# One all-engine barrier at the end of each phase, with GpSimd's semaphore clears after it: a two-layer hybrid decoder kernel

## The chip, the core and the metric

The kernel runs on one core of a Trainium2 chip. A core has five engines that run their own instruction streams and meet only at semaphores: TensorE (PE; its weight loads are listed as PEld), VectorE (DVE), ScalarE (ACT), GpSimd (POOL) and SyncE (SP), which here issues nearly all DMA transfers. The metric is the device time of one execution in microseconds (us), less is better. Durations of single instructions and waits come from one profiled execution of the kernel before.

## What is computed

Two causal decoder layers over a sequence of 1024 tokens, width 1024. Layer 0 mixes tokens with chunked gated linear attention (GLA), layer 1 with a dilated window attention in three head groups; beside each mixer runs a cross-attention into 256 memory tokens; each layer ends with a gated MLP. Cut to what matters:

```python
def reference(x, mem, ...):
    mem_n = rms_norm(mem, mem_norm)
    for i in range(DEPTH):                      # DEPTH = 2
        h = rms_norm(x, mix_norm[i])
        if i % 4 == 0:
            tok, xq = gla_mixer(h, a_w_in, a_w_gate2, a_b_gate, a_o_norm)
        else:
            tok, xq = dilated_mixer(h, b_w_in, b_q_norm, b_k_norm, positions)
        xa = memory_cross_attention(xq, mem_n, xa_w_kv[i], xa_q_norm[i], xa_k_norm[i])
        x = x + jnp.concatenate([tok, xa], axis=-1) @ w_out
        x = x + conv_ffn(rms_norm(x, ffn_norm[i]), ffn_w_up[i], ffn_conv_w[i], ffn_conv_b[i],
                         ffn_w_down[i])
    return x
```

All products are of float32 quality: a helper `split_matmul` (lines 50 to 52) makes each of three matmuls, high by high, high by low and low by high part.

## The kernel before

The program is a chain of twelve **phases**, each a Python function called from `build`, that follow each other in time: `project_phase` p0 (layer 0's input projection, with the memory's keys and values), `gla_phase`, `out_phase` o0 (output projection and norm), `ffn_phase` f0, then for layer 1 three pairs of `project_phase` p1_0, p1_1, p1_2 and `attention_phase` da0, da1, da2 (one pair per dilation), `out_phase` o1 and `ffn_phase` f1.

In each phase every engine has its own program, written inside one `nc.Block()`. Within a phase the engines are ordered by semaphores, one per kind of event (a tile loaded, split, turned, added). They only count up, and each phase counts from zero, so a phase's semaphores have to be back at zero before their numbers are handed out again. The allocator goes round the numbers, so that a number freed by one phase comes up again only after many others. Line 40 makes such a semaphore and leaves its clear as work for the end of the phase:

```python
def phase_semaphore(nc, ctx, name):
    s = ctx.enter_context(nc.semaphore(name))
    ctx.callback(nc.gpsimd.sem_clear, s)
    return s
```

What `ctx`, an `ExitStack`, does when the phase's `with` ends runs in the reverse of the order in which it was entered. So the end of a phase is: first the end of the `nc.Block()`, which is itself an all-engine barrier; then one clear on GpSimd for each semaphore of the phase; and last what was entered first, which before the change is `nc.all_engine_barrier`. A barrier has two halves: each engine drains and adds to a gather semaphore, GpSimd waits for the four others and then raises a release semaphore on which each of them waits (an EVENT_SEMAPHORE in the trace, whose start is the moment of the release). All of this has the line of the `with` that ends: L869 in a projection, L1396 in the GLA phase, L565 in an output phase, L82 in an MLP phase, L1141 in an attention phase. Two more `ExitStack`s have a barrier of their own: `c4` around p0 (L2405, 30 clears of the opening, the rope tables and the first parts), and `slots_ctx` around layer 1's weight slots (L2474, 6 clears, closed between p1_2 and da2).

What stands at a phase's start matters as well. In the GLA phase GpSimd first fills a mask `gla_keep` (L1563), which VectorE reads in a scan (L1705). At the end of da2 SyncE stores the last logarithms of the softmax sums, `group_lse<-stage_lse` (L2278), without waiting for them; o1 begins with SyncE waiting for that store and loading all three groups back, `o_logs<-group_lse` (L1944), with ScalarE issuing the load of the norm's gain, and with VectorE splitting two weight chunks (`o_w_lo`, L515), which wait for that gain, and then merging the groups (`o_top`, L1965, up to `XY`, L1988), for which TensorE waits.

Of the kernel before, what the change touches and what calls it, by code (L numbers as in the profile page):

```python
# [37 lines left out]


def phase_semaphore(nc, ctx, name):  # L40

    s = ctx.enter_context(nc.semaphore(name))
    ctx.callback(nc.gpsimd.sem_clear, s)
    return s
# [33 lines left out]
def ffn_phase(nc, ph, psum, ident, neg_half, X, hT_hi, hT_lo, w_up, conv_w, conv_b, w_down, x_out, raws, up, next_gain=None, next_w=None):  # L78
# [1 line left out]


    with ExitStack() as ctx:  # L82
        ctx.callback(nc.all_engine_barrier)
        def sb(name, shape, dt=F32):
            return ctx.enter_context(nc.sbuf_tensor(f"{ph}_{name}", shape, dt))

# [474 lines left out]
def out_phase(nc, ph, psum, ident, neg_half, XY, weights, x_dram, gain, out_hi, out_lo, w_up, up, raws, stage=None):  # L561
# [1 line left out]

    chunks, w_split = weights.chunks, weights.split
    with ExitStack() as ctx:  # L565
        ctx.callback(nc.all_engine_barrier)
        def sb(name, shape, dt=F32):
            return ctx.enter_context(nc.sbuf_tensor(f"{ph}_{name}", shape, dt))

# [263 lines left out]
def project_phase(nc, ph, psum, ident, neg_half, blocks, slots, extra_loads=(), guest=None, saves=None,  # L833
# [33 lines left out]
            n_heads += blk["kind"] == "heads"  # L867

    with ExitStack() as ctx:  # L869
        ctx.callback(nc.all_engine_barrier)  # L870
        def sb(name, shape, dt=F32):
            return ctx.enter_context(nc.sbuf_tensor(f"{ph}_{name}", shape, dt))

# [257 lines left out]
def attention_phase(nc, ph, psum, ident, units, stage=None, loads=(), load_unit=0, ahead=None, room=()):  # L1131
# [7 lines left out]
    U = len(units)  # L1139
    staged = TT * DIL_HEADS if stage is not None else 0  # L1140
    with ExitStack() as ctx:  # L1141
        ctx.callback(nc.all_engine_barrier)
        def sb(name, shape, dt=F32):
            return ctx.enter_context(nc.sbuf_tensor(f"{ph}_{name}", shape, dt))

# [239 lines left out]
def gla_phase(nc, ph, psum, ident, neg_half, hT_hi, hT_lo, w_in, w_gate2, b_gate, rank_rows, V, Y, room, first_parts, last_rows, cross_room, pieces,  # L1385
# [8 lines left out]
    DK, DV, PAIRS, CH = GLA_DK, GLA_DV, SEQ // P, SEQ // CHUNK  # L1394
    LAST = GLA_HEADS - 1
    with ExitStack() as ctx:  # L1396
        ctx.callback(nc.all_engine_barrier)
        def sb(name, shape, dt=F32):
            return ctx.enter_context(nc.sbuf_tensor(f"{ph}_{name}", shape, dt))

# [889 lines left out]
def build(nc, a, out):  # L2290

    with ExitStack() as ctx:
# [67 lines left out]
        with ExitStack() as c:  # L2360
# [11 lines left out]
            with ExitStack() as c2:  # L2372
# [12 lines left out]
                with ExitStack() as c3:  # L2385
                    slots = WeightSlots(nc, c3, "w0", B)

                    keys = [raws.tiles[1][:, :].rearrange("p (h n) -> p h n", h=XA_HEADS), sb("keys1", [P, XA_HEADS, N_MEM], F32, c3)]
                    vals = [raws.tiles[0][:, i * D // 2:(i + 1) * D // 2].rearrange("p (c n) -> p c n", c=2) for i in range(2)]
                    mem_parts = mem_hi, mem_lo  # L2390
                    def key_dest(i):
                        def dest(t, src):
                            s = src.rearrange("p (a n) -> p a n", n=P)
                            tok = slice(t * P, (t + 1) * P)
                            return [(keys[i][0:64, 0:XA_HEADS:2, tok], s[0:64, :, :]), (keys[i][64:P, 1:XA_HEADS:2, tok], s[64:P, :, :])]
                        return dest

                    kv_blocks = []
                    for i in range(2):
                        wkv = a["xa_w_kv"][i, :, :]  # L2400
                        kv = dict(tiles=N_MEM // P, stat=mem_parts, pick=plain)
                        kv_blocks += [dict(kind="heads", dim=XA_DIM, gain=xa_gain[i][1][:, :], w=wkv[:, 0:D_XA], dest=key_dest(i), **kv),
                                      dict(kind="copy", w=wkv[:, D_XA:2 * D_XA], dest=lambda t, i=i: vals[i][:, t, :], **kv)]
                    blocks[2:2] = kv_blocks
                    with ExitStack() as c4:  # L2405
                        c4.callback(nc.all_engine_barrier)
                        saves = [(keys_d[i], keys[i][:, :, :].rearrange("p h n -> p (h n)")) for i in range(2)]
                        saves += [(vals_d[i], vals[i][:, :, :].rearrange("p h n -> p (h n)")) for i in range(2)]

                        first = FirstParts(nc, c4, w, [XY[:, :, D_MIX + i * P:D_MIX + (i + 1) * P] for i in range(2)], qk_hi, qk_lo)  # L2410
                        rope = Rope(nc, c4, a["positions"], a["inv_freq"], XY[:, :, D_MIX:], *rope_d, first)
                        opening = Opening(
                            nc, c4, psum, ident, neg_half, band, split, zeros, [k[:, :, :] for k in keys],
                            [(xa_gain[i][j][:, :], a[f"xa_{n}_norm"][i, :]) for i in range(2) for j, n in enumerate("qk")]
                            + [(o_gain[:, :], a["a_o_norm"]), (dil_gain[0][:, :], a["b_q_norm"]), (dil_gain[1][:, :], a["b_k_norm"])],
                            a["mem"][0, :, :], a["x"][0, :, :], XY, [V[:, :, B + i * P:B + (i + 1) * P] for i in range(2)],
                            [xqT[:, i, :].rearrange("p (d n) -> p d n", d=DC) for i in range(2)], a["mem_norm"], a["mix_norm"][0, :],
                            *mem_parts, h0_hi, h0_lo)
                        project_phase(nc, "p0", psum, ident, neg_half, blocks, slots, guest=rope, saves=(5, saves), opening=opening)
# [22 lines left out]
        with ExitStack() as c:  # L2442
            cos, sin = sb("cos", [P, TT, DIL_DIM // 2], F32, c), sb("sin", [P, TT, DIL_DIM // 2], F32, c)
            rope_loads = [(x[:, :, :].rearrange("p t k -> p (t k)"), d) for x, d in zip((cos, sin), rope_d)]
            qT, kT = (sb(f"dil_{n}T", [P, DIL_HEADS, SEQ], F32, c) for n in "qk")
            V = XY[:, :, 0:D_DIL]
            XQ = XY[:, :, D_DIL + D_XA:]
            slots_ctx = c.enter_context(ExitStack())
            slots_ctx.callback(nc.all_engine_barrier)
            slots = WeightSlots(nc, slots_ctx, "w", HALF, raws)  # L2450

            def head_dest(x):
                return lambda t, src: [(x[:, :, t * P:(t + 1) * P], src.rearrange("p (h n) -> p h n", n=P))]

            def group_blocks(g):

                off, r = g * D_DIL, DILATIONS[g]
                blocks = [dict(whole, kind="heads", dim=DIL_DIM, gain=dil_gain[i][:, :], rope=(cos, sin), w=w[:, i * cols + off:i * cols + off + D_DIL],
                               pick=plain, dest=head_dest(x)) for i, x in enumerate((qT, kT))]
                return blocks + [dict(whole, kind="copy", w=w[:, 2 * cols + off:2 * cols + off + D_DIL],  # L2460
                                      pick=lambda x, d, t: tokens(x[:, d, :], t, r), dest=lambda t: V[:, t, :])]

            for g, r in enumerate(DILATIONS):
                blocks = group_blocks(g)
                if g == 0:
                    blocks.insert(0, dict(whole, kind="heads", dim=XA_DIM, gain=xa_gain[1][0][:, :], w=xq_w,
                                          pick=plain, dest=lambda t, src: [(XQ[:, t, :], src)]))
                project_phase(nc, f"p1_{g}", psum, ident, neg_half, blocks, slots, rope_loads if g == 0 else (),
                              room=raws.tiles)
                with ExitStack() as c2:  # L2470
                    if g + 1 < len(DILATIONS):
                        ahead = SlotsAhead(slots, group_blocks(g + 1)[0]["w"])
                    else:
                        slots_ctx.close()  # L2474
                        ahead = weights = OutWeights(nc, c1, "o1", (D_DIL + D_XA) // P, a["b_w_out"], raws, 3)
                    units = []
                    for t in range(TT):
                        for h in range(DIL_HEADS):
                            k, n, first = keys_of(kT[:, h, :], t, r)
                            mask = split[:, :] if r == 16 else band[:, 2 * P - n:2 * P]  # L2480
                            units.append((tokens(qT[:, h, :], t, r), k, n, mask,
                                          [V[:, first + i, h * P:(h + 1) * P] for i in range(n // P)],
                                          stage.tile[t % 2][:, h * P:(h + 1) * P], float(DIL_DIM) ** -0.5))
                    loads = ()
                    if g == 0:
                        keys, vals = xa_keys(1, c2)
                        loads = xa_loads(1, keys, vals)
                        units += xa_units(lambda h, t: XQ[:, t, h // 2 * P:(h // 2 + 1) * P], keys, vals, D_DIL)
                    attention_phase(nc, f"da{g}", psum, ident, units, stage, loads, TT * DIL_HEADS,
                                    ahead=ahead, room=raws.tiles if g + 1 < len(DILATIONS) else ())  # L2490
# [33 lines left out]
```

## Time and profile before

| what | us |
|---|---|
| median of 3 runs | 2705.37 (2704.56 to 2706.03) |
| the profiled execution's own time | 2706.76 |
| its span, first to last instruction | 2704.9 |
| TensorE (PE) busy | 2596.7 (96%) |
| VectorE, ScalarE, GpSimd busy | 1317.2, 845.6, 185.9 |
| mean granted TensorE clock | 0.98 |

The span is read against the profiled execution's own time, which is 1.9 us longer, and that again lies 1.4 us above the median of the runs. Semaphore instructions, drains and clears don't count as busy, so a stretch in which every engine only waits at a barrier shows as a stretch without any busy time.

### The profile page before, as it was taken

What the parts mean: (1) busy time and instruction counts of PE and PEld (TensorE: products, weight loads), DVE (VectorE), ACT (ScalarE), POOL (GpSimd) and SP (SyncE); (2) the same over time, 40 slices, a digit from 0 to 9 for tenths busy, and PEclk for the clock granted to TensorE, in tenths of its full rate; (3) what the DMA queues carried; (4) which work ended last, traced back from release to release, by engine and by line L of the source; (5) the groups of instructions that cost most, each with busy time, mean ns of one, the idle gap of its engine ahead of it and who ended that gap; (6) DMA issues with size and microseconds to landing.
All of it is one profiled execution on the core that took longest, in us unless ns stands there. A gap on an engine that the chain in (4) does not pass through costs nothing. (4 is left out here: it accounts for less than half of the span.)

```text
span 2704.9 us, 33076 instructions
## 1 busy us (share of the span) xinstructions
PE 2596.7 (96%) x12444; PEld 2201.6 (81%) x12444; DVE 1317.2 (49%) x2306; ACT 845.6 (31%) x1782; POOL 185.9 (7%) x263
## 2 busy tenths in 40 slices
PE   7998888999999999998999999997999999999999
PEld 7997767888888888887888888796778888888887
DVE  4423463354445555545545553443645444544455
ACT  6434342332222222224326433324332222222221
POOL 1100120000000000002211111111000000000000
PEclk9999898999999999998999999998999999999999
DMA  4221301131111111102102001103421111111111
GB/s 145 89 71 26 99 6 50 36 96 47 47 47 51 50 47 47 47 32 101 58 6 75 32 32 55 55 16 103 140 65 55 60 49 47 49 52 47 47 39 63
DMA packets 165245, 153.88 MB, mean 57 GB/s; under 512 B 32856, under 2 KB 135496, under 8 KB 165128
## 3 DMA queue, kind: packets, MB, share of 16 engines
q1 hardware_dynamic: 160968, 152.31, 17.7%
q8 instruction: 72, 1.18, 0.2%
q10 hardware_dynamic: 4160, 0.02, 0.1%
q14 instruction: 45, 0.37, 0.1%
HBM read 134.69 MB, written 17.61 MB: 56 GB/s over the span
## 5 line engine op out<-in xcount | busy, mean ns | idle before, releaser
L356 PE MATMUL psum<-hT_hi,f_up_hi 128*128 128x512 f32 x1376 | 426.7, 389 | 4.6 <-PEq L565 3.9
L356 PE MATMUL psum<-hT_hi,f_up_lo 128*128 128x512 f32 x1376 | 426.3, 389 | 0.0
L356 PE MATMUL psum<-hT_lo,f_up_hi 128*128 128x512 f32 x1376 | 426.2, 389 | 0.0
L238 DVE TENSOR_TENSOR f_up_lo<-raw,f_up_hi 128x1024 fp32r<-128x1024 f32 x84 | 102.9, 1225 | 490.6 <-ACT f_up_hi L182 490.6
L356 PEld LDWEIGHTS psum<-hT_hi,f_up_hi 128*128 128x128 f32 x1376 | 258.1, 188 | 59.4 <-issue 5.9
L356 PEld LDWEIGHTS psum<-hT_hi,f_up_lo 128*128 128x128 f32 x1376 | 258.3, 188 | 53.8
L356 PEld LDWEIGHTS psum<-hT_lo,f_up_hi 128*128 128x128 f32 x1376 | 258.3, 188 | 53.6
L256 DVE TENSOR_TENSOR XY<-XY,psum 128x512 f32<-128x512 f32 x352 | 234.4, 684 | 113.9 <-PE psum L52 113.7
L182 ACT ACTIVATE f_up_hi<-raw 128x1024 fp32r<-128x1024 f32 x84 | 89.1, 1061 | 614.6 <-PE psum L356 589.0
L50 PE MATMUL psum<-w_hi,hT_hi 128*128 128x512 f32 (+1 forms) x640 | 250.0, 391 | 17.0 <-DVE w_lo L808 10.5
L50 PE MATMUL psum<-f_down_hi,f_act_hi 128*128 128x512 f32 x640 | 249.0, 389 | 0.0
L51 PE MATMUL psum<-f_down_lo,f_act_hi 128*128 128x512 f32 x640 | 249.0, 389 | 0.0
L52 PE MATMUL psum<-f_down_hi,f_act_lo 128*128 128x512 f32 x640 | 249.0, 389 | 0.0
L52 PE MATMUL psum<-w_hi,hT_lo 128*128 128x512 f32 (+1 forms) x640 | 246.1, 385 | 0.0
L51 PE MATMUL psum<-w_lo,hT_hi 128*128 128x512 f32 (+1 forms) x640 | 246.0, 384 | 0.0
L50 PEld LDWEIGHTS psum<-w_hi,hT_hi 128*128 128x128 f32 x640 | 138.8, 217 | 35.7 <-DVE w_lo L808 10.1
L52 PEld LDWEIGHTS psum<-w_hi,hT_lo 128*128 128x128 f32 x640 | 138.8, 217 | 18.1
L51 PEld LDWEIGHTS psum<-w_lo,hT_hi 128*128 128x128 f32 x640 | 139.1, 217 | 16.7
L52 PEld LDWEIGHTS psum<-f_down_hi,f_act_lo 128*128 128x128 f32 x640 | 120.1, 188 | 25.0
L51 PEld LDWEIGHTS psum<-f_down_lo,f_act_hi 128*128 128x128 f32 x640 | 120.1, 188 | 24.9
L50 PEld LDWEIGHTS psum<-f_down_hi,f_act_hi 128*128 128x128 f32 x640 | 120.1, 188 | 24.9
L50 PE MATMUL psum<-w_hi,h_hi 128*128 128x384 f32 (+1 forms) x320 | 106.1, 332 | 2.3 <-DVE h_lo L475 1.7
(296 smaller groups left out, 4019.5 us busy)
## 6 DMA issues: line engine op xcount, KB each, us to landing
raw<-in_ffn_w_up_dram SPq DMA_DIRECT2D x88, 512.0 KB, 3.7
f_down_raw<-in_ffn_w_down_dram SPq DMA_DIRECT2D x22, 1024.0 KB, 4.9
w_raw<-in_b_w_in_dram SPq DMA_DIRECT2D x18, 1024.0 KB, 5.0
w_raw<-in_a_w_in_dram SPq DMA_DIRECT2D x8, 768.0 KB, 5.8
group_out<-stage SPq DMA_DIRECT2D x24, 256.0 KB, 2.3
o_outs<-group_out SPq DMA_DIRECT2D x24, 256.0 KB, 3.5
XY<-in_x_dram SPq DMA_DIRECT2D x8, 512.0 KB, 10.2
w_raw<-in_xa_w_kv_dram SPq DMA_DIRECT2D x8, 512.0 KB, 3.6
```

The lines of the kernel that those rows point to most:

```text
L50: nc.tensor.matmul(out, lhs_hi, rhs_hi, start=start, stop=False)
L51: nc.tensor.matmul(out, lhs_hi, rhs_lo, start=False, stop=False)
L52: return nc.tensor.matmul(out, lhs_lo, rhs_hi, start=False, stop=stop)
L182: nc.scalar.activation(up_hi[n_slot][:, :, :], up_raw[n_slot], ACT.Copy).then_inc(up_high, 1)
L238: nc.vector.tensor_tensor(up_lo[n_slot][:, :, :], up_raw[n_slot], up_hi[n_slot][:, :, :].bitcast(F32), ALU.subtract).then_inc(up_split, 1)
L256: nc.vector.tensor_tensor(xs, xs, psum[:, 4 + i % 4, :], ALU.add).then_inc(x_added, 1)
L356: mm = nc.tensor.matmul(psum[:, 2 * j + half, :], w[j][:, d, :], h[:, d, half * HALF:(half + 1) * HALF], start=first, stop=final)
```

## The change

The seven lines that leave a barrier as the last thing of a scope go. Two of them are in scopes that `build` opens once, five in phase functions that are called twelve times in all, so that 14 barriers leave the program. The barrier that ends each `nc.Block()` stays, and so do all 265 clears, in the same order on GpSimd: 21 of them end the program, and 17 (of scopes that had no barrier of their own: 6 behind p0, 6 behind o0, 5 behind o1) stand behind the last barrier of their place in the program before, too.

```diff
@@ def ffn_phase, gla_phase, out_phase, project_phase, attention_phase
     with ExitStack() as ctx:
-        ctx.callback(nc.all_engine_barrier)
         def sb(name, shape, dt=F32):
...
@@ def build
                     with ExitStack() as c4:
-                        c4.callback(nc.all_engine_barrier)
                         saves = [(keys_d[i], keys[i][:, :, :].rearrange("p h n -> p (h n)")) for i in range(2)]
...
             slots_ctx = c.enter_context(ExitStack())
-            slots_ctx.callback(nc.all_engine_barrier)
             slots = WeightSlots(nc, slots_ctx, "w", HALF, raws)
```

No instruction that computes or moves data changes its place on any engine; what goes is seen where an instruction waits for the barrier's gather semaphore. On GpSimd, between its last work of p0 (the norm's `p_head_rstd`) and its first of the GLA phase, an ISA row being one or more clears, the program before reads:

```order
L1017 TENSOR_TENSOR p_head_rstd<-p_head_sums,neg_half 128x4 [waits p0_mean]
L869 UNCONDITIONAL_BRANCH
L869 ISA [waits barrier_Pool_Activation_PE_DVE_SP_gather]
L869 ISA x12
L2405 ISA [waits barrier_Pool_Activation_PE_DVE_SP_gather]
L2405 ISA x29
L2385 ISA [waits barrier_Pool_Activation_PE_DVE_SP_gather]
L2385 ISA x5
L1561 UNCONDITIONAL_BRANCH
L1563 MEMSET gla_keep 96x1024
```

and the changed program at the same place:

```order
L1016 TENSOR_TENSOR p_head_rstd<-p_head_sums,neg_half 128x4 [waits p0_mean]
L869 UNCONDITIONAL_BRANCH
L869 ISA [waits barrier_Pool_Activation_PE_DVE_SP_gather]
L869 ISA x12
L2402 ISA x30
L2382 ISA x6
L1558 UNCONDITIONAL_BRANCH
L1560 MEMSET gla_keep 96x1024
```

Three barriers became one, the first; the 49 clears stand behind it, and no other engine waits for them. Between da2 and o1 the program before has, again on GpSimd, 11 clears (L1141) between two barriers:

```order
L547 TENSOR_TENSOR o_w_lo<-raw,o_w_hi 128x1024 [waits gla_xa_turned]
L1141 UNCONDITIONAL_BRANCH
L1141 ISA [waits barrier_Pool_Activation_PE_DVE_SP_gather]
L1141 ISA x10
L654 UNCONDITIONAL_BRANCH [waits barrier_Pool_Activation_PE_DVE_SP_gather]
L431 TENSOR_SCALAR o_norm_sums<-o_norm_sums 128x1 [waits gla_k_parked]
```

and the changed one has the same without the second wait (semaphores stand under the first name that their number had):

```order
L548 TENSOR_TENSOR o_w_lo<-raw,o_w_hi 128x1024 [waits gla_xa_turned]
L1140 UNCONDITIONAL_BRANCH
L1140 ISA [waits barrier_Pool_Activation_PE_DVE_SP_gather]
L1140 ISA x10
L654 UNCONDITIONAL_BRANCH
```

## Rows read from the trace of the kernel before

**Rows 1.** The page: span, and its first section, busy time per engine.

```profile
span 2704.9 us, 33076 instructions
PE 2596.7 (96%) x12444; PEld 2201.6 (81%) x12444; DVE 1317.2 (49%) x2306; ACT 845.6 (31%) x1782; POOL 185.9 (7%) x263
```

**Rows 2.** Instructions of line L1396, end of GLA: count, ns, first and last start.

```profile
L1396 POOLq EVENT_SEMAPHORE_RANGE_CLEAR  x38: 44/44/44, 412.3 to 415.2; - x38
L1396 PEldq EVENT_SEMAPHORE  x2: 51/51/51, 412.3 to 415.5; - x2
```

**Rows 3.** Windows between first and last release: length, busy per engine, PEclk, DMA share, GB/s.

```profile
216.70:220.30 3.60, 0.00 (x0) 0.00 (x0) 0.00 (x0) 0.00 (x0) 0.00 (x0) 0.75 0.00 0
412.30:415.50 3.20, 0.00 (x0) 0.00 (x0) 0.00 (x0) 0.00 (x0) 0.00 (x0) 0.50 0.01 3
533.50:534.90 1.40, 0.00 (x0) 0.00 (x0) 0.00 (x0) 0.00 (x0) 0.00 (x0) 1.00 0.00 0
1259.10:1261.30 2.20, 0.00 (x0) 0.00 (x0) 0.00 (x0) 0.00 (x0) 0.00 (x0) 0.50 0.00 0
1433.20:1434.40 1.20, 0.00 (x0) 0.00 (x0) 0.00 (x0) 0.00 (x0) 0.00 (x0) 1.00 0.00 0
1509.00:1510.00 1.00, 0.00 (x0) 0.00 (x0) 0.00 (x0) 0.00 (x0) 0.00 (x0) 1.00 0.00 0
1651.60:1652.80 1.20, 0.00 (x0) 0.00 (x0) 0.00 (x0) 0.00 (x0) 0.00 (x0) 1.00 0.00 0
1698.90:1699.90 1.00, 0.00 (x0) 0.00 (x0) 0.00 (x0) 0.00 (x0) 0.00 (x0) 1.00 0.26 8
1844.60:1846.80 2.20, 0.00 (x0) 0.00 (x0) 0.00 (x0) 0.00 (x0) 0.00 (x0) 0.98 0.00 0
1881.00:1882.10 1.10, 0.00 (x0) 0.00 (x0) 0.00 (x0) 0.00 (x0) 0.00 (x0) 0.50 0.48 158
1989.30:1991.20 1.90, 0.00 (x0) 0.00 (x0) 0.00 (x0) 0.00 (x0) 0.00 (x0) 1.00 0.00 0
sum 20.00, PE 0.00 PEld 0.00 DVE 0.00 ACT 0.00 POOL 0.00; mean PE 0.00 PEld 0.00 DVE 0.00 ACT 0.00 POOL 0.00
```

**Rows 4.** Instructions of lines L82 and L2292, the program's end.

```profile
L82 PEldq EVENT_SEMAPHORE  x2: 51/51/51, 2703.2 to 2704.8; - x2
L82 POOLq EVENT_SEMAPHORE_RANGE_CLEAR  x19: 44/44/44, 2703.2 to 2704.5; - x19
...
L2292 POOLq EVENT_SEMAPHORE_RANGE_CLEAR  x2: 44/44/44, 2704.8 to 2704.9; - x2
```

**Rows 5.** Instructions that write or read the tile gla_keep.

```profile
L1705 DVE TENSOR_TENSOR_SCAN raw<-gla_keep,gla_soft x4: 2287/2287/2287, 238.8 to 348.9; 96x1024 f32<-96x1024 f32 x4
L1563 POOL MEMSET gla_keep<- x1: 947/947/947, 220.8 to 220.8; 96x1024 f32 x1
```

**Rows 6.** The start of o1: DMA issues by line, line L1944, and the timeline.

```profile
group_lse<-stage_lse SPq DMA_DIRECT2D x1, 16.0 KB, 1.9
...
L1944 SPq DMA_DIRECT2D o_logs<-group_lse x3: 372/576/770, 1882.2 to 1883.2; - x3
DMA to landing us min/median/max: 2.9/3.1/3.5
...
1885.59 2.36 DVE L515 TENSOR_TENSOR o_w_lo<-raw,o_w_hi 128x1024 fp32r<-128x1024 f32 x2 [5.74 <-DMA o_gain<-in_ffn_norm_dram]
1887.87 0.18 DVE L1965 TENSOR_TENSOR o_top<-o_logs 128x32 f32<-128x32 f32 x1
```

**Rows 7.** Windows at half TensorE clock behind five boundaries, and one at full clock.

```profile
220.30:225.40 5.10, 5.02 (x16) 3.77 (x17) 0.00 (x0) 1.06 (x2) 1.07 (x2) 0.50 0.54 108
1437.10:1440.50 3.40, 3.40 (x12) 2.83 (x13) 1.46 (x11) 1.72 (x6) 0.00 (x0) 0.50 1.02 378
...
sum 22.10, PE 21.70 PEld 18.13 DVE 6.75 ACT 9.53 POOL 5.09; mean PE 4.34 PEld 3.63 DVE 1.35 ACT 1.91 POOL 1.02
...
534.90:540.00 5.10, 4.95 (x22) 4.12 (x23) 0.00 (x0) 0.00 (x0) 0.00 (x0) 1.00 0.27 42
```

More of the change, by code:

```diff
@@ L565, in out_phase @@
     with ExitStack() as ctx:
-        ctx.callback(nc.all_engine_barrier)
         def sb(name, shape, dt=F32):
@@ L869, in project_phase @@
     with ExitStack() as ctx:
-        ctx.callback(nc.all_engine_barrier)
         def sb(name, shape, dt=F32):
@@ L1141, in attention_phase @@
     with ExitStack() as ctx:
-        ctx.callback(nc.all_engine_barrier)
         def sb(name, shape, dt=F32):
@@ L1396, in gla_phase @@
     with ExitStack() as ctx:
-        ctx.callback(nc.all_engine_barrier)
         def sb(name, shape, dt=F32):
```

## The prediction, made before the change was timed

> **What bounds the kernel now.** I read the page first. TensorE is busy 96% of a span of 2704.9 us, and GpSimd 7% [rows 1]. With one engine so full, what a barrier costs is not the work of the barrier but the time in which TensorE cannot be fed; so the question is how long the whole core stands still at each of the twelve phase ends, and how much of that is the second barrier.
>
> The next view was the list of instructions by line, for the lines of the `with` statements. It lists semaphore instructions as well, though they don't count as busy. At the end of the GLA phase TensorE's queue is released twice, at 412.3 and at 415.5, and between the two GpSimd runs 38 clears that start from 412.3 to 415.2 [rows 2]. So one clear takes 2.9 / 37 = 0.08 us of GpSimd's time, though its own record is 44 ns long, and the barrier behind them takes 415.5 - 415.2 = 0.3 us with the last clear. The same reading at each other boundary gives a first and a last release, and the third view, the busy time in windows, was asked for just those stretches: in all eleven no engine has any busy time at all [rows 3]. They sum to 20.0 us. The stretches are as long as their clears are many: 3.6 us at the end of p0 (13 + 30 clears, two barriers), 1.0 to 1.2 us at the ends of projections and attentions.
>
> The reader is to see that everything of the next phase stands behind the last release. A stretch in which nothing works and nothing is awaited but the release can go completely, and everything after it moves earlier by its length.
>
> **The change part by part.**
>
> *The eleven inner boundaries.* After the change engines go on at the first release. Taken off: 3.6 + 3.2 + 1.4 + 2.2 + 1.2 + 1.0 + 1.2 + 1.0 + 2.2 + 1.1 + 1.9 = 20.0 us [rows 3], if nothing else holds the next phase back.
>
> *What could be awaited instead: a transfer.* If a DMA is under way in the stretch and its data is needed first, its landing doesn't move. The DMA share is 0.00 or 0.01 in nine of the eleven stretches; it is 0.26 at the end of da1 and 0.48 at the end of da2 [rows 3]. The one at da1 is again a store of that group's logarithms, which is read back only in o1, so nothing there waits. At da2 it matters: the store `group_lse` lands 1.9 us after it is issued, and SyncE's first load of `o_logs` starts at 1882.2, right with the last release at 1882.1 [rows 3, 6]. SyncE was held by the store about as long as by the barrier, and it will still start these three loads near 1882.2 to 1883.2. The last of them lands 2.9 to 3.5 us after its issue, at 1886.1 to 1886.7. VectorE takes them up at 1887.87, because until then it splits two weight chunks, whose start at 1885.59 waited for the gain that ScalarE loads right after the release [rows 6]. That part moves by the full 1.1 us, to 1886.8, which is still behind the landing. So I count the 1.1 us in full; if the landing comes late by a microsecond, all 1.1 is lost, and that is the bound.
>
> *What could be awaited instead: GpSimd.* Its clears now run beside the next phase's first work, up to 49 of them at the start of the GLA phase, 49 x 0.08 = 3.9 us. Before, GpSimd did the same clears and two more barriers ahead of its first work, so in absolute time it is never later than it was; it is only less far ahead of the others. Its first work there is the mask, at 220.8, read by VectorE at 238.8 [rows 5]. With VectorE 3.6 us earlier and GpSimd at least not later, 14 us of that distance are left. If that cover were gone, the clears' time, at most 3.9 us, would be paid again here. At the other boundaries GpSimd's first work waits for squared rows or for a weight load, which a phase produces only after work of its own. I put this at nothing.
>
> *The end of the program.* The last release pair is at 2703.2 and 2704.8, with 19 clears from 2703.2 to 2704.5, and two more clears close the program at 2704.9 [rows 4]. Here the clears are themselves the last work, and they don't go. At (2704.5 - 2703.2) / 18 = 0.07 us each, 21 of them take 1.5 us and end at 2704.7. Gain: 0.2 us, with 0 and the barrier's 0.3 as bounds.
>
> *TensorE's clock.* [...] In the 5.1 us behind the end of p0 TensorE is busy 5.02 us at 0.50, with ScalarE busy 1.06 and VectorE not at all, so TensorE sets the pace [rows 7]; it had just stood still over the 3.6 us of the stretch and some more. Behind o0, where the stretch is 1.4 us, the clock stays at 1.00 with 4.95 of 5.1 us busy [rows 3, 7]. After the change the standstill behind p0 is shorter by all of its 3.6 us and more like that of o0, so the half-clock stretch may not come at all: the 5.02 us would take half, a gain of 2.5 us. Five such stretches stand behind p0, p1_0, p1_1, da1 and p1_2, with 21.7 us of busy TensorE together [rows 7]. At full clock all five would take 10.9 us less, which is the upper bound of this term; nothing is the lower one, and a loss isn't excluded: behind the ends of o0 and o1 the clock is full now. If a stretch like the one behind p1_0, 3.4 us at half clock, came fresh behind both, 1.7 us would be lost at each, 3.4 us in all [rows 7]. I take 2.5 us, which is the first stretch alone: it is the one with the largest part of its standstill removed. In the three behind p1_0, p1_1 and da1 only 1.0 to 1.2 us goes, and I let them, p1_2 and any fresh ones cancel.
>
> [...]
>
> *The sum.* 20.0 + 0.2 + 2.5 = 22.7 us. Against the profiled execution, 2706.76 us by its own time (span 2704.9 and 1.9 around it), that is 2684.1; it lies 1.4 us above the median of the runs, and against the median 2705.37 - 22.7 = 2682.7 us, 0.84% faster.
>
> **The rivals.**
>
> *Only the barriers' own time goes.* If the next phase needs GpSimd, or the freed semaphores, from the start, then the clears stay on the path and only the 14 barriers at 0.3 us go: 4.2 us, 2701.2 us, which would read as no change. For it: the clears are by far the larger part of each stretch [rows 2]. Against: the distance of 18 us between the mask and its reader [rows 5]. [...]
>
> *The gain is partly taken back by the start of the phases.* Transfers that a phase issues first move with the release, so this needs one that doesn't: o1 (1.1 us), and no gain from the clock (2.5 us), with fresh half-clock stretches behind o0 and o1 (3.4 us). Together they give 2705.4 - 20.2 + 4.5 = 2689.7 us. For it: the DMA share in the stretch before o1. Against: the zeros in nine others.
>
> *The clears disturb the next phase: slower.* Of the program's 265 clears, 21 end it and 17 run behind a last release already, so 227 come to lie beside other engines' work. If each held up some engine on the path by 22.7 / 227 = 0.10 us, the change would end at nothing, and at 0.125 us each (28.4 us) at 2705.4 + 5.7 = 2711.1, slower. Against it: in the kernel before, 6 clears of p0's slots already run behind the last release beside the GLA phase's first matmuls, and 6 behind o0's, where TensorE is busy 4.95 of 5.1 us at full clock [rows 7]. A disturbance of 0.6 us would not fit into those 5.1 us.
>
> *The change does nothing at all*, because the end of a block is no full barrier or another one takes its place: the program's order shows one wait for the gather semaphore where there were two or three. I give it nothing.
>
> **How the numbers follow.** A measurement of this kernel can tell about 0.2%, 5.4 us, from no change. My forecast, the stretches gone and the clock between its bounds, has a chance of 0.84; the partly returned gain 0.08; barriers alone 0.04; more clock than I take, below 2677, 0.02; slower through the clears 0.02. The likeliest is 2682.7. The range goes down to 2677, by half of the clock term's remaining 8.4 us and some, and up to 2689, by the clock giving nothing and most of the losses of the second rival. Faster by over 0.2%: 0.94, same: 0.04, slower: 0.02.
>
> **What would show it.** Right: each phase end has one release, and TensorE's first load or the first DMA stands some 0.1 us behind it; the span is shorter by 20 us or more; GpSimd's clears lie beside TensorE's busy time; o1's load of `o_logs` starts about 1 us behind the release. The clock term: no half-clock stretch at the start of the GLA phase. Wrong: a new wait on GpSimd high in the list of waits, a gap between release and first work of more than it was, or matmuls of one shape that take longer while clears run.

## The result, and the profile after

The changed kernel takes 2682.56 us (median of 4 runs, 2682.13 to 2683.02), the kernel before 2705.7 us (four runs: the three of the table ahead of the prediction and one more of 2713.36); the ratio is 0.9912 with a 95% interval of 0.9895 to 0.9929, so about 0.9% faster. The forecast was 2682.7 us. Taken again later (e9 below) the ratio was 0.991 (0.9895 to 0.9925).

The page of the changed kernel, to compare with [rows 1]:

```profile
span 2680.3 us, 32922 instructions
PE 2590.5 (97%) x12444; PEld 2196.3 (82%) x12444; DVE 1316.2 (49%) x2306; ACT 845.2 (32%) x1782; POOL 185.5 (7%) x263
```

The span is 24.6 us shorter. TensorE is busy 6.2 us less with the same number of matmuls, which is a first hint that a part of the gain is its clock and not the barriers.

The end of the GLA phase by instruction, which was [rows 2] (the `with` now stands in line 1394):

```profile
L1394 POOLq EVENT_SEMAPHORE_RANGE_CLEAR  x38: 44/44/44, 405.5 to 408.4; - x38
L1394 PEldq EVENT_SEMAPHORE  x1: 51/51/51, 405.5 to 405.5; - x1
```

One release in place of two, and the 38 clears take the same 2.9 us, now behind it.

What a release is can be read at this place in the kernel before, whose trace has two barriers there:

```profile
L1396 POOLq EVENT_SEMAPHORE  x4: 17/17/17, 412.1 to 415.5; - x4
L1396 SPq DRAIN  x2: 7/7/7, 340.7 to 412.4; - x2
L1396 ACTq DRAIN  x2: 14/330/647, 403.2 to 412.4; - x2
L1396 POOLq DRAIN  x2: 41/580/1119, 404.1 to 415.3; - x2
L1396 PEldq DRAIN  x2: 13/1282/2552, 409.2 to 412.4; - x2
L1396 DVEq DRAIN  x2: 19/171/323, 411.8 to 412.4; - x2
L1396 SPq EVENT_SEMAPHORE  x2: 17/17/17, 412.3 to 415.5; - x2
L1396 ACTq EVENT_SEMAPHORE  x2: 17/17/17, 412.3 to 415.5; - x2
L1396 DVEq EVENT_SEMAPHORE  x2: 21/21/21, 412.3 to 415.5; - x2
```

Each of the five engines has one DRAIN per barrier. The records also name the semaphores that they count and wait on. In the first barrier the drains of SyncE, ScalarE, TensorE and VectorE (at 340.7, 403.2, 409.2 and 411.8) each add one to semaphore 96, the gather semaphore; GpSimd's drain adds nothing. GpSimd's EVENT_SEMAPHORE that waits on 96 starts at 412.1, its next one raises semaphore 97 at 412.2, and the records of the four others that wait on 97 (TensorE's is in [rows 2]) all start at 412.3. In the second barrier the four drains stand at 412.4, GpSimd's own at 415.3, its wait at 415.4, its raise at 415.5 and the four records at 415.5. So those four start within 0.1 us of GpSimd's raise, and their start is taken as the release.

The windows of the same lengths behind the eleven inner releases, columns as in [rows 3]:

```profile
216.90:220.50 3.60, 3.46 (x20) 2.91 (x21) 0.00 (x0) 1.04 (x2) 0.03 (x1) 1.00 0.45 89
405.50:408.70 3.20, 1.94 (x8) 1.56 (x8) 0.00 (x0) 1.12 (x2) 0.00 (x0) 0.50 0.18 4
...
1246.70:1248.90 2.20, 0.00 (x0) 0.00 (x0) 1.04 (x1) 2.00 (x2) 0.00 (x0) 0.50 0.39 131
...
1858.20:1859.30 1.10, 0.00 (x0) 0.00 (x0) 0.00 (x0) 0.57 (x1) 0.00 (x0) 0.50 0.47 153
1966.80:1968.70 1.90, 1.75 (x8) 1.47 (x9) 0.00 (x0) 0.00 (x0) 0.00 (x0) 1.00 0.10 29
sum 20.00, PE 14.37 PEld 12.33 DVE 2.87 ACT 8.09 POOL 0.03; mean PE 1.31 PEld 1.12 DVE 0.26 ACT 0.74 POOL 0.00
```

Where there was no busy time at all in 20.0 us, TensorE now works 14.4 of them while GpSimd clears. In two rows TensorE still has nothing to do. Behind f0, at 1246.7, ScalarE and VectorE start on the next phase's input at once, and TensorE's first matmul came forward with them, from 4.7 to 2.5 us behind the first release. Behind da2, at 1858.2, SyncE is held by the store of `group_lse`, and what became of that is told under e5, e6 and e11.

The program's end, to compare with [rows 4], takes 1.5 us from the first release to the end of the last clear, where it took 1.7:

```profile
L84 POOLq EVENT_SEMAPHORE_RANGE_CLEAR  x19: 44/44/44, 2678.9 to 2680.2; - x19
...
L84 PEldq EVENT_SEMAPHORE  x1: 51/51/51, 2678.9 to 2678.9; - x1
...
L2289 POOLq EVENT_SEMAPHORE_RANGE_CLEAR  x2: 44/44/44, 2680.2 to 2680.3; - x2
```

With the stretches gone, what is left of the 24.6 us is seen by measuring each phase from the last release ahead of it to the first one behind it. "Half clock" is the time in the phase at which the profile shows a granted clock of 0.5:

| phase | before, us | after, us | half clock in it, before and after, us |
|---|---|---|---|
| GLA | 192.0 | 188.6 | 38, 29 |
| f0 | 724.1 | 723.1 | 6, 4 |
| p1_0 | 171.9 | 171.0 | 9, 7 |
| da1 and da2 | 80.3 | 79.8 | 10, 4 |
| o1 | 107.3 | 108.6 | 19, 20 |
| the six others | 1406.9 | 1407.1 | 15, 15 |

So 20.0 us are stretches, 0.2 the end, 5.8 shorter phases with less time at half clock, and 1.3 and 0.2 are lost again in o1 and elsewhere: 24.6 before rounding. Between the medians the gain is 23.1 us, less by 1.5: the profiled execution of the kernel before, 2706.76 us, lies 1.1 us above its median, and that of the changed one, 2682.13, 0.4 below. The experiments show which part of the phases' 5.8 us belongs to the change.

### The profile page after: what moved, and what is told of

It is laid out like the page before. It is cut to its first block and busy times, and to the rows that moved or that the text cites. A ratio compares the mean times of both kernels' runs of the same rounds, so it can differ in the third digit from the quotient of the medians.

```text
span 2680.3 us, 32922 instructions
## 1 busy us (share of the span) xinstructions
PE 2590.5 (97%) x12444; PEld 2196.3 (82%) x12444; DVE 1316.2 (49%) x2306; ACT 845.2 (32%) x1782; POOL 185.5 (7%) x263
```

## The experiments

### e1 and e2: is a stretch made of the barrier or of the clears?

In e1 the second barrier is registered just ahead of the block and so runs ahead of the clears:

```diff
-        ctx.callback(nc.all_engine_barrier)
         def sb(name, shape, dt=F32):
...
+        ctx.callback(nc.all_engine_barrier)
         block = ctx.enter_context(nc.Block())
```

> The kernel before with all its barriers, but the second one of each scope stands ahead of the clears instead of behind them, so that the clears lie beside the next phase's first work. Theory A (the stretch is the clears, a bare second barrier costs 0.3 us): 13 inner barriers at 0.3 us on top of the changed kernel's 2682.6, so 2686.5 us (2685 to 2688), and no stretch without work over 0.5 us between two releases. Theory B (what costs is that all engines meet a second time, about 1 us and more each, whatever GpSimd does in between): near the kernel before, 2695 to 2705 us.

Measured: 2686.42 us, ratio 0.9928 (0.9911 to 0.9945). At the end of the GLA phase, by instruction:

```profile
L1396 POOLq EVENT_SEMAPHORE_RANGE_CLEAR  x38: 44/44/44, 404.1 to 407.0; - x38
...
L1396 PEldq EVENT_SEMAPHORE  x2: 51/51/51, 403.8 to 404.1; - x2
```

The two releases are 0.3 us apart, where they were 3.2. It is so at ten of the twelve places; at p0 and at p1_2, where the inner scope's 13 clears still stand ahead of the outer scope's barrier, they are 1.5 us apart. Theory A holds; theory B had 2695 us and more. (That the median lies within 0.1 us of theory A's number is luck: the four runs spread from 2682.5 to 2690.2.)

In e2 both barriers stay and neighbouring semaphores of a scope are cleared by one instruction:

```diff
-    ctx.callback(nc.gpsimd.sem_clear, s)
+    (first semaphore of the scope) ctx.callback(clear_runs, nc, numbers)
...
+        nc.gpsimd.sem_clear(range(nums[0], nums[0] + n))
```

> The kernel before with both barriers of each scope, but one clear instruction for each run of neighbouring semaphore numbers (about 20 instructions in place of 265). Theory A: each stretch shrinks from its 1.0 to 3.6 us to about 0.4 us (p0 and p1_2, with one barrier more, 0.8), 20.0 - 5.2 = 14.8 us off, 1.4 us off at the program's end, and about 2 us of clock: 2687 us (2685 to 2690). Theory B: at most the end's 1.4 us, 2704 us. Rival to A: a clear costs by the number of semaphores in it, then nothing changes, 2705 us.

Measured: 2689.41 us, ratio 0.9933 (0.9916 to 0.995). All clears of the program, the GLA phase's 38 semaphores in one of them, and that phase's releases:

```profile
L49 POOLq EVENT_SEMAPHORE_RANGE_CLEAR  x23: 45/86/242, 217.3 to 2692.3; - x23
...
L1412 PEldq EVENT_SEMAPHORE  x2: 51/51/51, 413.0 to 413.5; - x2
```

The longest clear, that of the 38 semaphores, takes 242 ns, so 38 at once cost less than a tenth of 38 one by one, and the releases are 0.5 us apart in place of 3.2. The clears are the cost, told from the other side. Of the 23.1 us that the change gives, this kernel gives some 17 without taking any barrier away.

### e3 and e4: do clears beside other work cost anything?

```diff
+    for _ in range(4):          (two in e3)
         ctx.callback(nc.gpsimd.sem_clear, s)
```

> The changed kernel with each clear issued twice, 530 in place of 265. If clears beside other engines' work cost nothing but GpSimd's own time: 21 more at the program's end at 0.07 us, 2684.1 us (2683 to 2685.5). If each clear holds up an engine on the path (the slower rival): 227 more at 0.1 us, about 2705 us. GpSimd's mask in the GLA phase is written about 3.8 us later, 7.3 us behind the release, still ahead of its reader.

> The changed kernel with each clear issued four times. The cover used up: at the start of the GLA phase 196 clears at 0.078 us keep GpSimd for 15.3 us, so the mask is ready 16.4 us behind the release, where VectorE wants it 15 to 17 us behind it: 0 to 1.5 us lost there; at the start of da2 GpSimd's first split comes up to 2 us late, which nothing waits for; at the end 63 more clears, 4.4 us. Sum 2682.6 + 4.4 + 0.7 = 2687.7 us (2686.5 to 2690). If clears disturb other engines: 2682.6 + 3 x 22 = about 2750 us.

Measured: 2683.19 us for e3, ratio 0.991 (0.9894 to 0.9927), and 2689.67 us for e4, ratio 0.9933 (0.9916 to 0.9949). Twice the clears cost nothing beside other work that the runs show, and the slower rival, which needed 22 us more, is out. (At the program's end, where the clears are the last work, e3's profile has 3.0 us in place of 1.5; the median is only 0.6 above the changed kernel's.) The profiles say it more sharply than the times: VectorE's first instruction of the GLA phase stands 14.9 us behind the release with 3 clears beside TensorE's work (e10), with 49 (the changed kernel) and with 98 (e3). Four times the clears find the edge of the cover. VectorE's first instruction of the GLA phase in e4, in the timeline:

```profile
232.61 1.22 DVE L1702 SCALAR_TENSOR_TENSOR gla_soft<-raw,gla_soft 96x1024 f32<-96x1024 f32 x1 [15.65 <-POOL gla_keep L1563]
```

It is released by GpSimd's mask now, not by ScalarE. The release was at 217.2, so it starts 15.4 us behind it, against 14.9 in the changed kernel: 0.5 us of wait. Of the 7.1 us in the median 4.4 are the program's end (5.9 us behind the last release in the profile against 1.5). The 2.2 us that these two leave are put down to the scatter shown under e9, which one profile and four runs don't prove.

### e7 and e8: the clock behind the end of p0

e7 puts the two barriers at the end of p0 back into the changed kernel; e8 takes these two alone out of the kernel before. In both the edit is a condition on the phase's name and the line in `c4`:

```diff
+        if ph == "p0":          (e8: if ph != "p0")
             ctx.callback(nc.all_engine_barrier)
```

> The changed kernel with the two removed barriers at the end of p0 back. Stretch alone: 3.6 us slower, 2686.2 us. With the clock term of the forecast (a half-clock stretch of 5 us of busy TensorE at the GLA phase's start comes back): 6.1 us slower, 2688.7 us, and the granted clock shows half behind the GLA phase's first matmuls. If the clock effects later in the GLA phase are luck of position, they scatter by 1 to 3 us either way.

> The kernel before with only the two barriers at the end of p0 removed. Stretch alone: 3.6 us faster, 2701.8 us. With the clock term: 6.1 us faster, 2699.3 us, and full granted clock in the first 5 us of the GLA phase.

Measured: e7 2687.84 us (6 runs), ratio 0.9927 (0.9915 to 0.9939), 5.3 us more than the changed kernel's first median; e8 2702.33 us (11 runs), ratio 0.998 (0.9972 to 0.9989), 5.3 us less than the kernel before beside it (2707.65). Both lie between the bare stretch (3.6) and the stretch with the clock term (6.1), but the times can't choose: e8's interval is 3.0 to 7.6 us and holds both, and against the kernel before of its own batch e7 gives 19.8 us, where the changed kernel gave 23.1 and again 24.6, which is 3.3 to 4.8 us of difference. The windows choose. The changed kernel, then e7, over the GLA phase's first 5.1 us:

```profile
217.00:222.10 5.10, 5.06 (x27) 4.24 (x28) 0.00 (x0) 1.06 (x2) 1.07 (x2) 1.00 0.55 108
```

```profile
220.20:225.30 5.10, 5.07 (x18) 3.82 (x19) 0.00 (x0) 1.07 (x2) 1.07 (x2) 0.56 0.56 108
```

The changed kernel gets through 27 matmuls at full clock where e7 gets through 18, nearly all at half, and the kernel before through 16 [rows 7]. What it is worth can be read free of everything later, by the start of VectorE's first instruction of the GLA phase. The kernel before (last release at 220.3), the changed one (216.9), e7 (220.1) and e8 (217.1):

```profile
237.54 1.22 DVE L1704 SCALAR_TENSOR_TENSOR gla_soft<-raw,gla_soft 96x1024 f32<-96x1024 f32 x1 [21.03 <-ACT gla_soft L1618]
```

```profile
231.85 1.22 DVE L1701 SCALAR_TENSOR_TENSOR gla_soft<-raw,gla_soft 96x1024 f32<-96x1024 f32 x1 [15.14 <-ACT gla_soft L1615]
```

```profile
237.16 1.22 DVE L1703 SCALAR_TENSOR_TENSOR gla_soft<-raw,gla_soft 96x1024 f32<-96x1024 f32 x1 [20.82 <-ACT gla_soft L1617]
```

```profile
232.06 1.22 DVE L1705 SCALAR_TENSOR_TENSOR gla_soft<-raw,gla_soft 96x1024 f32<-96x1024 f32 x1 [15.18 <-ACT gla_soft L1619]
```

It stands 17.2, 14.9, 17.1 and 15.0 us behind the release. In the nine other kernels it is 14.9 to 15.0 in seven, 15.4 in e4 for the wait told above, and 16.6 in e2, where the two barriers with few clears left 0.9 us between the first and the last release and the clock fell for 3.4 us. So this clock term is 2.1 to 2.3 us, and it comes and goes with the barriers.

### e5, e6 and e11: what o1 lost

In the changed kernel VectorE is ready to merge the groups 1.7 us sooner behind the first release, but it then waits:

```profile
1865.46 0.40 DVE L1972 TENSOR_TENSOR o_logs<-o_logs,o_inv 128x32 f32<-128x32 f32 x3
1868.33 0.88 DVE L1983 TENSOR_SCALAR XY<-o_outs,o_logs 128x128 f32<-128x128 f32 x4 [2.48 <-DMA o_outs<-group_out]
```

The last of the three loads of the first tile's groups landed 5.7 us after its issue, against 3.2 in the kernel before. This wait is not there in the kernel before, nor in e6 and e8, which have the barrier behind da2 too: VectorE's own work ends at 9.2 to 9.6 us behind the first release there, and the load has landed by 7.7 to 8.4. In the ten other profiles VectorE is ready at 7.4 to 7.7 us and starts only when the load has landed, at 7.6 to 10.1. So with the barrier gone, or short as in e1 and e2, this load is what the start of o1 waits for, in every execution profiled. Between the two kernels the load of a weight chunk behind it came 1.0 us earlier, which gave theory C. e5 moves it behind the second tile's loads:

```diff
                 merge.load(sp, 0)
+                merge.load(sp, 1)
                 for k in range(max(weights.ahead + 2, chunks - 1), chunks):
                     weights.load(sp, k)
-                merge.load(sp, 1)
```

> The changed kernel; in o1 SyncE issues the 512 KB load of a weight chunk after the three loads of the second token tile instead of ahead of them. Theory C (in the changed kernel that weight load comes 1.0 us earlier and shares the DMA queues with the first tile's third load, which lands 10.0 us behind the release in place of 7.7 less 1.0): that load lands by 7.7, VectorE's merge starts at about 7.9 us behind the release in place of 10.1, and TensorE's first work at 11.2 in place of 13.4; time 2.0 us less than the changed kernel, 2680.6 us. If the weight chunk itself is then late for TensorE, 0 to 1 us. Rival D (the load waits for the store of the last logarithms, which a release can't move): nothing changes, 13.4 and 2682.6 us.

> The changed kernel with the second barrier back at the end of da2 alone. Theory C: the stretch of 1.1 us comes back, but the weight load is again later than the first tile's loads, so TensorE's first work in o1 stands 11.6 us behind the second release, 12.6 behind the first, against 13.4 in the changed kernel: 0.7 us faster than the changed kernel, 2681.9 us. Theory D (the store binds and nothing else): the same time, 2682.6. Plain count of stretches: 1.1 us slower, 2683.7.

e11 makes SyncE wait with everything behind the first tile:

```diff
                 merge.load(sp, 0)
+                sp.wait_ge(merge.loaded[0], 48)
                 for k in range(max(weights.ahead + 2, chunks - 1), chunks):
                     weights.load(sp, k)
```

> The changed kernel; in o1 SyncE waits until the first token tile's three loads have landed before it issues the weight chunk and the second tile's loads. If the transfers issued behind them delay the first tile's third load (3.2 to 5.7 us from issue to landing so far, whatever the order of those behind), it now takes 3.2 us or less and lands 7.5 us behind the release, VectorE's merge starts at 7.7 and TensorE at 11.0 in each execution. If its landing is late for another reason, it still scatters from 7.5 to 10. The time gains at most 1.5 us, and the second tile or the weight chunk, now 3 us later, may take it back.

Measured: e5 2684.18 us, ratio 0.991 (0.9896 to 0.9923); e6 2683.39 us, 0.9911 (0.9898 to 0.9924); e11 2684.57 us, 0.9903 (0.9886 to 0.9919). None is told from the changed kernel by its time. Counted from the first release at the end of da2, in each profile:

| kernel | third load lands, us | TensorE's first work in o1, us |
|---|---|---|
| barrier behind da2: before, e6, e8 | 7.7, 8.2, 8.4 | 12.6, 12.9, 12.6 |
| a short one, 0.3 to 0.4 us: e1, e2 | 7.5, 7.8 | 10.9, 11.1 |
| none: changed, e3, e4, e7, e9, e10 | 10.0, 8.6, 8.8, 7.7, 7.6, 7.9 | 13.4, 11.9, 12.2, 11.0, 11.0, 11.3 |
| none, weight chunk last: e5 | 9.2 | 12.6 |
| none, all behind held back: e11 | 7.8 | 11.1 |

Theory C fails as it was put: with the weight chunk out of the way the load of e5 still landed at 9.2, and TensorE started at 12.6 where the theory had 11.2. (e6's 12.9 is near theory C's 12.6, but so is that of the kernel before, which has the same barrier.) The store does hold SyncE, as was forecast (1.1 us behind the release in each), but that alone costs nothing: e7, e9 and e10, whose o1 is the same up to its clears, start TensorE at 11.0 to 11.3 where the changed kernel's profile has 13.4. The mean without the barrier is 11.8 us over the six kernels of the third row, against 12.7 with it, so about 0.9 of the 1.1 us is kept on the mean, and the profiled execution of the changed kernel was an unlucky one by 1.6. e11 agrees with the view that the transfers issued behind it delay the load, but it took 3.5 us from issue to landing, not 3.2 or less, and so little sets it off from e7, e9 and e10 that one profile doesn't settle it. Why the load is late in some executions stays open.

### e9 and e10: the changed kernel again, and with range clears

> The changed kernel once more, beside the two below on the same chip. Ratio to the kernel before 0.991 to 0.992. If the half-clock stretches inside the GLA phase fall by position and not by the change, the GLA phase's length in the profile again lies anywhere from 185 to 195 us and follows the time spent at half clock; TensorE's first work in o1 lies 11 to 13.4 us behind the release.

> The changed kernel with one clear instruction for each run of neighbouring semaphore numbers. The clears beside other work cost nothing, so taking them away gains nothing there; at the program's end two or three clears stand in place of 21: 1.3 us less than the changed kernel in the same batch. If clears did disturb others: 2 us and more beyond that.

e10 has the edit of e2 on top of the changed kernel. Measured: e9 2682.16 us, ratio 0.991 (0.9895 to 0.9925); e10 2680.25 us, 0.9896 (0.9881 to 0.9911). e10 is 1.9 us below e9, where 1.3 was expected, with runs that spread over 2675.9 to 2683.7. In its profile 0.3 us lie between the last release and the end, in place of 1.5. It has the lowest median of all kernels here, though the runs alone don't tell it from the changed one.

What spreads the runs is seen in the GLA phase's windows, from release to release. Columns as before; the one behind POOL is the granted clock. e1, the changed kernel, e9 and e3 (the kernel before lies between the last two, with 192.0 us at 0.90):

```profile
218.60:403.80 185.20, 164.20 (x872) 131.37 (x872) 98.07 (x176) 84.32 (x209) 29.83 (x30) 0.94 0.16 48
```

```profile
216.90:405.50 188.60, 167.68 (x872) 133.74 (x872) 98.18 (x176) 84.84 (x209) 29.22 (x30) 0.92 0.16 47
```

```profile
216.60:407.20 190.60, 169.67 (x872) 135.37 (x872) 98.24 (x176) 84.91 (x209) 29.99 (x30) 0.91 0.15 46
```

```profile
216.90:411.80 194.90, 173.96 (x872) 139.37 (x872) 99.32 (x176) 84.67 (x209) 29.80 (x30) 0.89 0.15 45
```

The same 872 matmuls take TensorE from 164.2 to 174.0 us. Over the thirteen profiles the time at half clock in this phase runs from 23 to 44 us, and the phase's length goes with it at 0.46 us for each (correlation 0.99): 174.9 us and 0.46 for each us at half clock. Where in the phase the clock falls differs from execution to execution of the same code, as between the changed kernel, where it is granted 1.00 from 250 to 300 us, and e9, where it is granted 0.97 there; only the stretch at its very start goes with the barriers.

## Why the prediction was right

*The stretches, 20.0 us:* right, and for the reason given. The releases are single, TensorE works in them, and e1 and e2 show from two sides that it was the clears, at 0.08 us each, and hardly the barriers, at 0.3, that made them long.

*GpSimd's delay, nothing:* right. e3 adds as much again and e4 finds where it ends: between 7 us and 14.3 us of clears ahead of the mask. The forecast put the cover at 14 us, from the start of the mask to the scan that reads it; measured the same way it was 12.6, since the better clock brings VectorE forward by 2.3 us, and GpSimd, rid of two barriers, comes to the mask 0.5 us sooner behind the first release. What waits for the mask, though, is the instruction ahead of the scan, as e4 shows, and to that one it was 11.4 (14.9 us behind the release, less 3.5 for the clears), the mask's own 1.1 us not counted.

*The program's end, 0.2 us:* 0.2 in the profile.

*The clock, 2.5 us behind p0:* shown in kind and size. It measured 2.1 to 2.3 us, in the start of VectorE's work in thirteen profiles. (The GLA phase is 3.4 us shorter in the changed kernel's profile; what goes beyond this term lies inside the phase's scatter.) The other stretches were taken to cancel. Fresh half-clock stretches behind o0 and o1, which the second rival feared, came in none of the thirteen profiles. In f0, p1_0 and da1 with da2 the changed kernel's profile has 2.4 us less; the profiles of e3 to e11 other than e8, which all lack most of the barriers, have the same or nearly so in f0 (722.6 to 722.9 against 724.1) and p1_0 (171.1 to 171.3 against 171.9), while their da1 is 45.8 to 46.4 against 46.1. That these 2 us in f0 and p1_0 belong to the change was not tested by itself, and e8, which has f0's barriers, has 170.7 in p1_0. The standstill behind p1_0 shrank to 0.9 us and the half-clock stretch still came in the changed kernel, which speaks against the far end of 10.9 us; in e9 it did not. In the nine profiles in which the hole at this place, from TensorE's last matmul of one phase to its first of the next, is 0.9 us, the stretch came in four, and behind p1_1, with the same hole, in six. At p0 the hole went from 5.0 to 1.4 us and the half-clock stretch went with it; for the other places the traces give no rule.

*o1, 1.1 us in full:* the sum's weakest step. The wait on the store was seen in the rows and judged rightly as nearly harmless for `o_logs` (0.2 us of wait in the changed kernel's profile); what was not looked at is the load behind it, `o_outs`, which VectorE needs 2.5 us later, and whose landing had only 0.7 us to spare at the forecast time (it landed at 7.7 us, VectorE would have been there at 8.3). VectorE came at 7.4 to 7.7, sooner than forecast, and waited for that load each time. Measured over the profiles about 0.9 of the 1.1 us came; in the profiled execution TensorE started 0.8 us later behind the first release than before.

*The rivals:* that only the barriers' own time goes (2701.2) and that clears disturb others (2711.1) are both excluded, by the time itself and by e1 and e3. The forecast's argument against the second, that 0.6 us would not fit into a window busy for 4.95 of 5.1 us, was weak, since a disturbance could also lie in longer matmuls; e3 and e10 close it. The gain partly taken back was there in o1, in part of the executions, at the size of a microsecond.

That the forecast and the median differ by 0.1 us is luck. Some 2 us in f0 and p1_0 were not counted, the clock behind p0 was counted 0.2 to 0.4 us too high and o1 about 0.2, and single runs spread by several us. Against the median of the kernel before that the result has, 2705.7 us, the forecast gain of 22.7 us is 0.4 short of the 23.1 measured.

## What to carry to other kernels

Count the instructions that stand between two barriers on the one engine that does them: here a bare barrier cost 0.3 us and each semaphore clear 0.08 us for all five engines, so 38 clears cost ten barriers. Work of that kind either goes behind the last barrier, where an engine with slack has it for nothing until its own first consumer comes (98 clears ahead of the mask cost nothing that the runs show, 196 cost VectorE 0.5 us of wait), or into one instruction for a range (38 semaphores in 242 ns). Clears may go behind the last barrier only if their numbers are not counted on again before the clears have run; here the order in which numbers are handed out takes care of it. And a stretch of standstill removed ahead of a TensorE-bound start can pay twice, once for itself and once by the clock that no longer falls: 3.6 and 2.1 to 2.3 us behind p0, and nothing certain behind the other phases.

When a start moves forward, check not only the first transfer that it waits for but the one behind it: its spare time was 0.7 us here, and in all ten profiles in which VectorE came forward it was the transfer that VectorE waited for.

## What the runs showed of the hardware

- One clear of a single semaphore is a 44 ns record, but a new one starts only each 0.07 to 0.08 us. A clear of a range took 45 to 242 ns, the longest being that of 38 semaphores.
- The GLA phase of one and the same program took 188.6 and 190.6 us, and over thirteen nearly equal programs 185.2 to 194.9 us, all of it in step with 23 to 44 us at half clock. Medians of four or five runs of this kernel can't settle 2 us; the start of one named instruction behind a release agreed to 0.1 us in nine of the thirteen profiles.
- The half-clock stretch of 3.4 us behind p1_0 and p1_1 came behind holes of 0.9 us between matmuls in ten of eighteen cases (nine profiles, two places each) and not in the other eight.
- The third of three equal 256 KB loads, issued 0.5 us behind the second, landed 3.2 to 5.7 us after its issue in the same program order.
